# Attention inside a two-layer backbone: two global jobs' scores side by side in five PSUM banks, the shares left unscaled, and the output scaled per query and turned back

## What is computed

```
# global: 128 queries a block, 640 keys (512 latent, 128 of a cache) for latent tokens
s = einsum('bqgrd,bkgd->bgrqk', q_blk, k) * scale
p = softmax(s, axis=-1)
return einsum('bgrqk,bkgd->bqgrd', p, v)
# neighbourhood: a band of keys with a learned bias, and 128 cached keys
p = softmax(concatenate([s_band, s_ctx], axis=-1), axis=-1)
o = einsum(p[..., :n_band], vg) + einsum(p[..., n_band:], v_ctx)
```

## Time and profile before

| | us |
|---|---|
| median of 3 runs | 3347.34 |
| lowest and highest | 3344.22, 3348.79 |
| profiled execution: its own time | 3349.19 |
| its span in the trace | 3347.4 |
| attention, from its first score to its last weigh | 715.5 to 873.9 |
| PE busy over the span | 91% |
| mean granted clock of PE | 0.953 |

### The profile page before, as it was taken

One profiled execution on the slowest core, in us unless ns is written; L12 is line 12 of the kernel. 1 busy time (PEld: TensorE's weight loads), 2 busy tenths in 40 slices (PEclk: granted clock), 3 DMA queues, 4 the chain that ended last, 5 costly groups with the idle time before them and its releaser, 6 DMA issues.

```text
span 3347.4 us, 48972 instructions
## 1 busy us (share of the span) xinstructions
PE 3031.5 (91%) x20388; PEld 2860.8 (85%) x20388; DVE 1881.6 (56%) x2666; ACT 1036.3 (31%) x1646; POOL 363.2 (11%) x231
## 2 busy tenths in 40 slices
PE   2999999987889999999999999976777789999998
PEld 2999999965789999999999989972445579999998
DVE  7567666546665556566565553773555665632334
ACT  2311134447642111442112442331111234421123
POOL 1000012000110000210000200003643312000002
PEclk9999999999999999999999999996878879999999
DMA  4445443310234444434443343220000023322223
GB/s 175 158 148 181 150 154 126 113 53 11 92 107 158 142 130 156 134 111 158 142 139 117 122 140 118 76 76 13 26 13 13 29 86 107 120 90 69 76 90 119
DMA packets 97085, 354.49 MB, mean 106 GB/s; under 512 B 10848, under 2 KB 17120, under 8 KB 96096
## 3 DMA queue, kind: packets, MB, share of 16 engines
q1 hardware_dynamic: 91232, 342.31, 30.9%
q10 hardware_dynamic: 5632, 9.05, 0.8%
HBM read 339.65 MB, written 11.67 MB: 105 GB/s over the span
## 4 chain that ended last, share of the span: by engine, by line
PE 73%; DVE 14%; ACT 6%; issue 4%; POOL 2%; DMA 1%; ACTq 0%; DVEq 0%; SPq 0%; POOLq 0%
PE P L1459 63%; DVE cv L1361 3%; DVE wl L971 2%; ACT wh L677 2%; PE P L1597 2%; DVE em L1217 1%; PE P L1386 1%; PE P L1605 1%; ACT pb L784 1%; DVE st L1095 1%; DVE xs L1233 1%; DMA mraw<-wmod_d 1%; PE P L1645 1%; PE P L1648 1%; POOL nbuf L590 1%
## 5 line engine op out<-in xcount | busy, mean ns | idle before, releaser
L1459 PE MATMUL P<-xh,wh 128*128 128x320 f32 x4016 | 1020.2, 313 | 27.5 <-DVE xl L1010 16.7
L1459 PE MATMUL P<-xl,wh 128*128 128x320 f32 x4016 | 1010.5, 311 | 0.0
L1459 PE MATMUL P<-xh,wl 128*128 128x320 f32 x4016 | 1009.9, 311 | 0.0
L971 DVE TENSOR_TENSOR wl<-raw,wh 128x1024 fp32r<-128x1024 f32 (+1 forms) x431 | 567.8, 1318 | 419.4 <-ACT wh L677 418.5
L677 ACT CAST wh<-raw 128x1024 fp32r<-128x1024 f32 (+1 forms) x431 | 482.8, 1120 | 977.3 <-PE P L1459 852.8
L1459 PEld LDWEIGHTS P<-xh,wh 128*128 128x128 f32 x4016 | 700.9, 189 | 36.1 <-DVE xl L1010 19.1
L1459 PEld LDWEIGHTS P<-xl,wh 128*128 128x128 f32 x4016 | 700.6, 190 | 0.0
L1459 PEld LDWEIGHTS P<-xh,wl 128*128 128x128 f32 x4016 | 700.4, 189 | 0.0
L590 POOL TENSOR_TENSOR nbuf<-nbuf 128x320 f32<-128x320 f32 x108 | 168.3, 1562 | 2414.8 <-ACT nbuf L692 2414.8
L1459 PE MATMUL P<-hh,wh 128*128 128x320 f32 x1408 | 381.0, 311 | 0.0
L1459 PE MATMUL P<-hl,wh 128*128 128x320 f32 x1408 | 378.4, 309 | 0.0
(11 more groups left out here) (206 smaller groups left out, 2737.0 us busy)
## 6 DMA issues: line engine op xcount, KB each, us to landing
raw<-wgu_d SPq DMA_DIRECT2D x216, 512.0 KB, 3.4
mraw<-wmod_d SPq DMA_DIRECT2D x144, 512.0 KB, 3.3
raw<-wdB_d SPq DMA_DIRECT2D x64, 704.0 KB, 4.1
raw<-wdA_d SPq DMA_DIRECT2D x32, 704.0 KB, 5.0
raw<-ain_d SPq DMA_DIRECT2D x28, 512.0 KB, 3.2
raw<-sz_d SPq DMA_DIRECT2D x26, 512.0 KB, 3.3
raw<-sx_d SPq DMA_DIRECT2D x24, 512.0 KB, 3.2
raw<-aout_d SPq DMA_DIRECT2D x16, 512.0 KB, 3.2
```

The costliest lines, as they stand in the source:

```text
L971: V.tensor_tensor(wl[:, u.u % SPLITS, 0:n], raw[:, u.u % 2, 0:n], wh[:, u.u % SPLITS, 0:n].bitcast(F32), ALU.subtract).then_inc(lo_done, 1)
L1459: ins = nc.tensor.matmul(P[:, u.banks[i], 0:C], w[:, u.u % SPLITS, k * 128:(k + 1) * 128], m[:, k, C * h:C * h + C], start=(k == 0 and w i ...
```

## The change

Four things are altered, all in `attention(p)` and the functions it calls.

1. Scores. The global jobs alternate between columns 0 to 1279 and 1280 to 2559 of banks 0 to 4, so that bank 2 holds an end of both. `scores_of` becomes `scores_first`, issued two jobs ahead of the turns (for a global job the 640 columns' worth of work that needs only the job before last), and `scores_rest` for the remaining pieces (256 columns a head), behind the first exponential of the job before. An even global job makes its second head's exponential first (`head_order`).
2. Shares. Both forms of `shares` are gone. `pb` holds plain exponentials; these are turned, copied and weighed. DVE keeps the reciprocal (`one_over`).
3. Weighing. `ptr` (128 keys x 128 queries) is now the loaded weights and the values (64 columns) are streamed, one head after the other, so that the output has queries on the partitions. DVE's `scale` multiplies it by the reciprocals into `osc` (128x128), PE's `turn_back` transposes `osc`, and `take` reads that. Everything is in bank 7, so each `weigh` waits for the `take` of the job before.
4. Order and banks. Turned groups alternate between banks 5 and 6, over all jobs (`turn_bank`), so a group waits for the copy of the group before last; the third group of a global job reuses the bank of its first. PE's round n is: rest of the scores of n+1, `turn` n, `turn_back` n-1, first scores of n+2, `weigh` n. ACT's is copies of n, exponentials of n+1. DVE's is `scale` n-1, `front` n+1 (for the late jobs `front` n+2 behind `take`), `take` n-1, `one_over` n.

The diff, without declarations, unchanged lines and the body of what is removed (it is in the listing above):

```diff
@@ -425 +422 @@
         def score(job):
             if job.kind == "gl":
-                return P[:, 0:4, :].rearrange("p (a b) c -> p a (b c)", a=2)[:, :, 0:T]
+                c = 2 * T * (job.i % 2)
+                return P[:, 0:5, :].rearrange("p b c -> p (b c)")[:, c:c + 2 * T].rearrange("p (h c) -> p h c", h=2)
             b = 2 * (job.i % 2)
...
-        def out_bank(job):
-            return 7 if job.kind == "gl" else 6 + job.i % 2
+        def head_order(job):
+            return (1, 0) if job.kind == "gl" and job.i % 2 == 0 else (0, 1)
+        def turn_bank(g):
+            return 5 + g % 2
@@ -780 +783 @@
                     act.wait_ge(tr_done, jobs[i - 2].g1)
-                for h in range(2):
+                for h in head_order(job):
                     nc.scalar.activation(pb[:, i % 2, h, 0:job.n], score(job)[:, h, :], ACT.Exp, bias=st[:, 1, q, h:h + 1],
...
                                          accum_out=st[:, 2, q, h:h + 1]).then_inc(p_done, 1)
-            def shares(job):
...
-                    nc.scalar.activation(p, p, ACT.Copy, scale=st[:, 3, q, h:h + 1]).then_inc(pn_done, 1)
             def turn(job):
@@ -799 +795 @@
                     n = 128 * len(group)
-                    nc.scalar.copy(ptr[i % 2][:, 512 * q:512 * q + n], P[:, 4 + q, 0:n]).then_inc(ptr_done, 1)
+                    nc.scalar.copy(ptr[i % 2][:, 512 * q:512 * q + n], P[:, turn_bank(job.g0 + q), 0:n]).then_inc(ptr_done, 1)
             def attention(p):
@@ -814 +810 @@
                 load_bias(1)
-                for i in range(len(jobs) + 1):
...
-                        turn(jobs[i - 1])
+                for n in range(-1, len(jobs)):
+                    if n >= 0:
+                        turn(jobs[n])
+                    if n + 1 < len(jobs):
+                        nxt = jobs[n + 1]
+                        exps(nxt)
+                        if nxt.kind == "nl" and nxt.b == 3 and nxt.t < 2:
+                            load_bias(nxt.t + 2)
@@ -1096 +1091 @@
-            def shares(job):
+            def one_over(job):
                 i, q = job.i, job.i % 4
                 dve.wait_ge(p_done, 2 * i + 2)
-                rc = V.reciprocal(st[:, 3, q, :], st[:, 2, q, :])
-                if job.kind != "gl":
-                    rc.then_inc(rc_done, 1)
-                    return
-                me(rc)
+                me(V.reciprocal(st[:, 3, q, :], st[:, 2, q, :]))
+            def scale(job):
+                i, q = job.i, job.i % 4
                 me.wait()
-                for h in range(2):
-                    p = pb[:, i % 2, h, 0:job.n]
-                    V.tensor_scalar(p, p, st[:, 3, q, h:h + 1], None, ALU.mult).then_inc(pn_done, 1)
+                dve.wait_ge(pv_done, i + 1)
+                V.tensor_tensor(osc[:, :].rearrange("p (h c) -> p h c", h=2), P[:, 7, 0:128].rearrange("p (h c) -> p h c", h=2),
+                                bc_last(st[:, 3, q, :], HD), ALU.mult).then_inc(o_scaled, 1)
             def take(job):
                 i = job.i
-                o = P[:, out_bank(job), 0:128]
+                o = P[:, 7, 128:256]
                 if job.kind == "nl":
...
                     hi, lo = [queries(m[:, job.to, :], job) for m in (xh, xl)]
-                dve.wait_ge(pv_done, i + 1)
+                dve.wait_ge(o_turned, i + 1)
                 V.tensor_copy(hi, o).then_inc(o_hi, 1)
...
             def attention(p):
-                for i in range(len(jobs) + 2):
...
-                        take(jobs[i - 2])
+                near = 1 + sum(1 for job in jobs if job.kind == "gl")
+                for n in range(-1, len(jobs) + 1):
+                    if n >= 1:
+                        scale(jobs[n - 1])
+                    if n + 1 < near:
+                        front(jobs[n + 1])
+                    if n >= 1:
+                        take(jobs[n - 1])
+                    if near <= n + 2 < len(jobs):
+                        front(jobs[n + 2])
+                    if 0 <= n < len(jobs):
+                        one_over(jobs[n])
                 dve.wait_ge(kv_out, 32)
@@ -1462 +1465 @@
-            def scores_of(job):
+            def pieces(job, h):
+                base = 2 * T * (job.i % 2) + T * h
+                edges = sorted({0, LAT, T} | {512 * b - base for b in range(6) if 0 < 512 * b - base < T} | ({384} if base == 0 else set()))
+                out = []
+                for a, b in zip(edges, edges[1:]):
+                    rows = slice(64 * h, 64 * h + 64)
+                    keys = kc[rows, 0, a - LAT:b - LAT] if a >= LAT else pt[rows, job.tk, CTX + a:CTX + b]
+                    out.append(((base + a) // 512, slice(a, b), keys))
+                return out
+            def is_first(job, h, piece):
+                bank, cols, keys = piece
+                if job.i % 2 == 0:
+                    return cols.stop <= 384
+                return cols.start >= (256 if h == 0 else 128) and not (h == 1 and cols.start >= LAT)
+            def global_scores(job, first):
+                both = [[(h, x) for x in pieces(job, h) if is_first(job, h, x) == first] for h in range(2)]
+                for n in range(max(len(both[0]), len(both[1]))):
+                    for mine in both:
+                        if n < len(mine):
+                            h, (bank, cols, keys) = mine[n]
+                            ins = nc.tensor.matmul(score(job)[:, h, cols], queries(pt[64 * h:64 * h + 64, job.tq, :], job), keys,
+                                                   start=True, stop=True)
+                return ins
+            def scores_first(job):
                 i = job.i
                 if job.kind == "gl":
-                    pe.wait_ge(v_cp, 2)
-                    if i:
-                        pe.wait_ge(p_done, 2 * i)
-                else:
-                    pe.wait_ge(p_done, max(2 * (i - 1), 32))
+                    if i < 2:
+                        pe.wait_ge(v_cp, (2, 5)[i])
+                    else:
+                        pe.wait_ge(p_done, 2 * (i - 1))
+                    global_scores(job, True).then_inc(qk_first, 1)
+                    return
+                pe.wait_ge(p_done, 2 * (i - 1))
                 halves = [slice(64 * h, 64 * h + 64) for h in range(2)]
...
                 else:
-                    n = LAT if job.kind == "gl" else 2 * WIN
+                    n = 2 * WIN
                     for h, rows in enumerate(halves):
-                        keys = pt[rows, job.tk, CTX:T]
-                        if job.kind == "nl":
-                            keys = keys[:, 8 * WINDOW[job.b]:8 * WINDOW[job.b] + 2 * WIN]
+                        keys = pt[rows, job.tk, CTX + 8 * WINDOW[job.b]:CTX + 8 * WINDOW[job.b] + n]
                         nc.tensor.matmul(score(job)[:, h, 0:n], queries(pt[rows, job.tq, :], job), keys, start=True, stop=True)
...
                         ins = nc.tensor.matmul(score(job)[:, h, n:n + CTX], queries(pt[rows, job.tq, :], job),
-                                               kc[rows, 0 if job.kind == "gl" else 1 + job.t, :], start=True, stop=True)
+                                               kc[rows, 1 + job.t, :], start=True, stop=True)
                 ins.then_inc(qk_done, 1)
+            def scores_rest(job):
+                if job.i:
+                    pe.wait_ge(p_done, 2 * (job.i - 1) + 1)
+                pe.wait_ge(qk_first, job.i + 1)
+                global_scores(job, False).then_inc(qk_done, 1)
             def turn(job):
                 i = job.i
+                pe.wait_ge(p_done, 2 * i + 2)
                 for q, group in enumerate(job.groups):
-                    if job.before[q] is None:
-                        pe.wait_ge(v_cp, 5)
-                    else:
-                        pe.wait_ge(ptr_done, job.before[q] + 1)
-                    pe.wait_ge(pn_done, 2 * i + group[-1][0] + 1)
+                    g = job.g0 + q
+                    if g >= 2:
+                        pe.wait_ge(ptr_done, g - 1)
                     for c, (h, j) in enumerate(group):
-                        ins = nc.tensor.transpose(P[:, 4 + q, 128 * c:128 * c + 128], pb[:, i % 2, h, 128 * j:128 * j + 128], ident)
+                        ins = nc.tensor.transpose(P[:, turn_bank(g), 128 * c:128 * c + 128], pb[:, i % 2, h, 128 * j:128 * j + 128], ident)
                     ins.then_inc(tr_done, 1)
             def weigh(job):
@@ -1504 +1543 @@
                 if i >= 1:
-                    pe.wait_ge(o_done, i if job.kind == "gl" else i - 1)
+                    pe.wait_ge(o_done, i)
                 m = job.n // 128
-                for j in range(m):
-                    for h in range(2):
+                for h in range(2):
+                    for j in range(m):
                         cols = slice(64 * h, 64 * h + 64)
@@ -1520 +1559 @@
                         c = 128 * (m * h + j)
```

(34 more changed lines are left out.)

26 lines of the change are left out of this document (2 added, 24 removed).

## The result

The changed kernel took 3381.19 us (median of 6 runs, 3375.04 to 3386.70) against 3348.60 for the kernel before: ratio 1.0095, interval 1.0079 to 1.0111. It is slower, as forecast, but by 32.6 us, not by 20.2, and it lies 1.2 us above the upper end of the range. Its profiled execution took 3378.96, 29.8 more than the one before. Run again twice beside the experiments it gave 3372.82 (ratio 1.0072, interval 1.0057 to 1.0087) and 3379.62 (1.0098, 1.0084 to 1.0112). So the same program differs by 8 us from one group of runs to another, and its first figure is the highest of three; the two others lie inside the range. Within the first group the time goes with the mean granted clock of the run: 3375.04 at 0.951, 3386.70 at 0.947.

A forecast was written before the change was run, and what follows sets the result against it. PE bound the kernel as a whole, but in the attention no engine was full and chains of waits bound. Global +9.4, late +8.0, small +2.1 and end +0.7 gave 20.2 us more: 3367.5 median, range 3347 to 3380.

The forecast's parts named there:

- The price of a weighing record: Weighing on PE: each record costs 0.107 us by its load of 128 weight columns, 2.29 for a global job.
- PE's global round: Global jobs: PE's work sums to 5.52 us a round against 4.93 before, +9.4 us over 16 rounds.
- The late circle: Late jobs: a circle through DVE and PE (scale, turn back, scores, front) takes 3.57 us a round; four blocks add +8.0.
- ACT's product on the chain: Late jobs before the change: ACT's product of over 1.1 us a job lay on the chain of waits and goes.
- DVE's product of 1.0 a job goes off the chain: Global jobs: removing DVE's product of 1.0 us a job shortens its chain, an edit said to hide below PE.
- Small jobs and end: Rounds of `gc` jobs go from 1.63 to 2.15 us, four adding +2.1; `aout` waits +0.7 behind the last weighing.
- the term for the clock: Granted clock, first stretch: loss at 1.2 GHz and an earlier 2.4 GHz taken as equal; ends -1 and +5 us.
- Rival E: 1.2 GHz holds longer in rounds PE binds, or odd jobs' pieces run one by one: 3380 to 3390; chance 8%.
- C: Weighing: a record costs by its streamed columns, 0.055 us, so the global round is 4.5; 3348.5 us; chance 9%.
- B: Late jobs: the circle through DVE and PE doesn't close, rounds run at PE's 3.3 us; 3361 us; chance 14%.
- D: Global rounds: PE stops being the bound, its round falling under 4.93 us; faster, about 3330 us; chance 7%.

The follow-up runs named there:

- the filled kernel: Changed kernel with four idle transposes of the identity into bank 4 before the weighing of each small job; 3371.81 us.
- the five banks alone: Kernel before with the change's five banks and early scores for global jobs only, old weighing, late jobs as before; 3343.33 us against 3349.98, ratio 0.9981.

## Why the prediction was right and where it was wrong

- *The price of a weighing record.* 0.107 from the earlier trace rows; weighing took 2.35 for my 2.29. Right; put back to the old form it took 1.24.
- *PE's global round.* 5.52 against 5.73. Every term was a little low: rest 0.60 and 0.65, turns with bank wait 1.65 and 1.66, turn back 0.17 and 0.20, first scores 0.81 and 0.87, weighing 2.29 and 2.35. So a round rose by 0.81 and not by 0.59, over a third more. Twelve settled rounds gave +9.7; the first three together were 0.9 shorter than before, as the first fell from 6.1 to 3.6, where the second job's scores no longer wait for the exponentials of the first; and the last round's +0.8 is counted with the small rounds. That the sum of +8.8 lies so near the forecast +9.4 is thus partly luck. (The early pieces are 384 columns a head, as my sum has them; the description of the change says 640 columns' worth.)
- *The late circle.* 3.57 forecast, 3.57 measured, and the blocks +1.8 for +2.0. The mechanism held; that it fits to a hundredth is luck, as the turn back took 0.25 until the scores for my 0.17, and the steps from negation to scale 0.27 for my 0.34. That the cause named for the round before (ACT's product on the chain) was wrong did no harm, as the round after was built up from its own steps. In the earlier trace rows line 793 had 6.5%, too little for 1.14 us of 3.28; I should have taken that as the sign it was. In the global jobs the prediction says that "DVE's product of 1.0 a job goes off the chain", where its own reading of the earlier trace rows gives the products no share; the kernel without them kept its 4.92.
- *Small jobs and end.* 2.15 a round forecast and 2.2 measured at 2.4 GHz. The small rounds as a whole took +2.4 at 2.4 GHz (the filled kernel) and +3.1 with the slower clock; 0.8 of either is the last global round. The end took +1.1 for +0.7.
- **The step that failed is the term for the clock**, "I take the two as equal; ends -1 and +5". I sized it by the first stretch alone and named no place behind it. There the change won (0.9). The loss came in the small jobs and the first block, 20.5 us at 1.2 GHz where the kernel before had 6.8, and cost some 4.7 us: 5.8 in place of the 1.8 of the other blocks, and 0.7 in the small rounds. The kernel with its small jobs filled puts it at 5.7, as its first block (16.5) is shorter than the others. Rival E had the mechanism, a round bound by PE at 1.2 GHz, but named no place, and the paragraph on the clock looked only at the first stretch. Inside the attention 24.5 stand against 20.2, and this is the difference. The cost lies at the upper end of the -1 to +5 that I allowed, or just over it; why the clock falls there stays open.
- *Outside the attention.* 5.1 us more, which nothing lays to the change: whatever was done to the attention, these parts were up to 6.8 longer and 1.1 shorter than in the trace before. I had put nothing for it, and the three runs that I built on hid it (all runs of the kernel before lie between 3343.6 and 3354.5). So of the 12.4 us between the forecast 20.2 and the measured 32.6, 4.3 lie inside the attention, 5.1 outside, and 2.8 between profiled executions and medians. The first is the failed step; the others are spread, and the forecast's distance to the second group of runs (23.8 us slower) is only 3.6. (The kernel before, run again beside the changed one, is another 1.3 over the median that the forecast starts from.)
- *The rivals.* C fell with the price of the record, B with the circle. D fell with the same price. Its turning point was put at 0.08 a record; the two rounds measured, 5.73 at 0.11 and 4.62 at 0.055, put the 4.93 of before at 0.07, an estimate that takes the line between them as straight.
- *Direction and size.* Slower was right, and so was the ground for it: weighing with 128 loaded columns took 2.35 for 1.24 and became PE's longest step. The Trainium skill, "TensorEngine Tiling (Array Packing)", "When to Use Tiling", advises the swap that the change undid. The trace agrees: putting it back gave 1.11 a global round, and 18 us in all.

## What to carry to other kernels

Before a product is turned round so that a scale becomes cheap, count its loaded columns: here 128 loaded and 64 streamed cost 0.11 a record, 64 loaded and 128 streamed by two heads side by side 0.055, and the detour back brought a second circle between two engines. Make the parts of such a change one by one; the five banks alone were worth 6.6 us in their group of runs and 8.4 in the trace. Compare such parts by their rounds in the trace, as the totals of equal programs differ by more than many of them are worth. And when a stage becomes bound by PE, price its quiet corners at 1.2 GHz as well.

## What was not expected of the hardware

The granted clock fell to 1.2 GHz for 13.7 to 20.5 us in all three traces of the changed kernel, starting in small jobs in which PE worked with waits of 0.2 to 0.4 us between its groups, and stayed at 2.4 GHz when four transposes filled one of those waits. Why the variants without turn back or with the old weighing, which have gaps as well, kept 2.4 GHz there is not settled. What such a spell costs differs: 6.8 us at 1.2 GHz cost the kernel before some 0.8, 20.5 us cost the changed kernel 4.7 to 5.7, about twice as much for each microsecond of it (0.12 against 0.23 to 0.28). That this is because PE binds more of the changed rounds fits the rows at 1.2 GHz, but was not tested by itself.

One DMA issue on ACT lasted 0.70 us in one trace and 1.94 to 2.28 in twelve, and moved the whole stage by 1.3. And the same program gave medians of 3372.8, 3379.6 and 3381.2 in three groups of runs, 0.25% apart, so that a difference of 0.2% is less than what a single group can tell.
